# A hybrid decoder layer on one core: projections, pool sums and new tokens laid out anew in the first part

## The chip, the cores and the metric

The kernel runs on one core of a Trainium2 chip. The metric is device time in microseconds, from the start to the end of one execution, lower is better. All data is float32.

## The reference, cut to what matters

One layer for 256 prompt tokens and 8 sample tokens (one new token in each of 8 sequences that have 1024 cached positions):

```python
h = rmsnorm(x, norm_mix)
u, q, k, v, f_logit, g_logit = split(h @ w_in)          # 4 parts of 512 columns, 8 forget columns, 2 x 1024 gates
logf = log_sigmoid(f_logit + b_forget)
pooled[g] = window_sum(u, WINDOWS[g]) / count - u       # windows 2, 4, 8, 16 over time, 128 channels each
pool_out = (pooled @ w_pool) * pool_scale
att = softmax(q k^T / 8 + c_q - c_k, causal) v          # c = cumsum(logf); samples read paged k, v, logf
y = sig(g0) * (pool_out @ w_up_pool) + sig(g1) * (att @ w_up_att)
x = x + y @ w_out
x = x + hier_moe(rmsnorm(x, norm_ffn))                  # 4 groups of 8 experts, top-1 group, top-2 experts
out = rmsnorm(x, norm_final)                            # and new k, v, logf, pool rows
```

The pages of k and v are picked from a cache by a page table: 8 sequences x 8 pages of 128 rows. Each of the 32 experts has three matrices of 2 MB.

## The kernel before, in words

**Storage.** SBUF has a ring of nine slots of 2 MB. In the first part six of them (FRONT) take a stream of 2 MB loads, worked out by a planner: four column blocks of w_in (Q, K, V, U), four gate blocks of w_in, the K and V pages of each sample, w_up_pool, w_up_att and two halves of w_out. Slots 6 to 8 hold activations. SyncE issues weight loads (L485, L489), GpSimd's queue issues the indirect loads of the pages (L562), of the cached forget values (L551), the broadcasts of each sample's query (L574) and most small outputs. Every load waits until the last use of what its slot held.

**Order.** A list PLAN gives one order of steps; each engine runs through it and does its part of each step, in order. Steps: `proj` (L1224 to 1245) multiplies hT (tokens transposed, normalised) with a column block: for each of two blocks of 128 tokens hT is the stationary operand and 512 columns of w_in stream past (L1240); the eight samples are done before with 32 stationary columns in four column groups (L1230), copied by ScalarE and added up by a matmul (L1245). So q, k, v, u come out with tokens on the partitions; `qk` (L1271) transposes q and k back. `forget` (L1250) has 8 stationary columns. `pages` on VectorE sums the cached forget values, `bias` (L1264, L1265, L873) adds the sums over later pages. `keysN` (L879, L883) multiplies two pages of a sample's keys with its query on VectorE and sums over 64 dimensions; four such steps per sample, then L888 to L890. `dmax`, `dshift`, `dsums`, `dpv`, `dsum`, `datt` are the decode softmax of one sample: transpose of the maxima (L1276), shift (L1279, L896), exp (ACT L667), sums (L899), probabilities times V in four column groups (L1286), the new token's V row with 8 contraction rows (L1287), the total (L1290, L901), scaling (L907) and a sum over partitions (L1295). `head` is one prompt head: scores and bias (L1339, L1340), softmax (L923 to L927, ACT L692, L693), transposes of the probabilities of the head before (L1328), `pv` (L1346 to L1348). `pool` makes window sums as matmuls with band matrices (L1306 to L1310) and mixes them (L1314). `gate` (L1320) makes one of 16 tiles of gate logits, `up` and `merge` (L1359) multiply with w_up_pool and w_up_att, `out` (L1368, L1374) with w_out. One turn of the loop over the samples b = 1 to 8 has two gates, one sample's softmax, one head, one `up`.

**After the plan.** `norm` squares x (ACT L618), takes an inverse root in 13 small VectorE operations (L775 to L782), normalises (L786), transposes (L1142, L1145) and multiplies with the router. `route` picks experts; before expert 0 PE also gathers the tokens, and builds tables of slots (L1417, L1422). Then for each expert: gate and up (L1184), turning, down (L1200), combination into PSUM (L1211, L1213). Expert e's loads wait for expert e - 3: w_gate and w_up for its gate and up products (`s_gu`, L452), w_down for its down product (`s_dn`, L454). At the end the rows are squared (ACT L745, L748), a root is taken and two row blocks and the samples are scaled (L1119, L1121) and written (L532, L536).

**Start.** SyncE loads x_sample, small constants (`cea`), x_prompt, then the stream. GpSimd loads the page table in eight small loads that repeat each value on 16 partitions (L547); ScalarE loads the forget weights (L596, 1024 pieces of 32 bytes). x is squared on ScalarE, normalised on VectorE and then transposed on PE.

## Time and profile before

| | us |
|---|---|
| median of 3 runs | 801.41 (799.28 to 801.55) |
| the profiled execution, its own time | 802.27 |
| its span, first to last instruction | 800.5 |
| PE busy | 651.5 (81%) |
| VectorE busy | 250.7 (31%) |
| ScalarE busy | 71.2 (9%) |
| GpSimd busy | 44.6 (6%) |
| moved by DMA | 269.65 MB, mean 337 GB/s |

The times of stages below are offsets from the span's start. A matmul in float32 stands as two records; "x16" are eight matmuls. PEclk is the granted TensorE clock: 1.00 is 2.4 GHz, 0.50 is 1.2 GHz. The span and the execution's own time differ by 1.8 us, which lies around the span.

### The profile page before, as it was taken

To read this page: it belongs to the slowest core of one execution; us is meant where nothing else is said; L and a number is where in the kernel's file an instruction comes from. 1 tells how busy PE (TensorE), PEld (TensorE's weight loads), DVE (VectorE), ACT (ScalarE), POOL (GpSimd) and SP (SyncE) were. 2 spreads that over 40 slices of the span, in tenths; PEclk is the share of its full clock that TensorE was granted. 3 is DMA by queue.
4 is the path that set the end of the run, shared out by engine and by line. 5 is a ranking of instruction groups with operands and counts; after the bars stand their busy time and mean duration, and the time that the engine had idled before them with its cause. 6 is when DMAs were issued, how large, how long until landed. Compare 5 with 4: busy or idle time off the path is not lost.

```text
span 800.5 us, 13635 instructions
## 1 busy us (share of the span) xinstructions
PE 651.5 (81%) x6078; PEld 361.7 (45%) x6078; DVE 250.7 (31%) x634; ACT 71.2 (9%) x182; POOL 44.6 (6%) x55
## 2 busy tenths in 40 slices
PE   1999989999999997899787778677778668778673
PEld 1334476566666635544343344334434334344341
DVE  3104639788782325622111111111111111111103
ACT  2012121111111010100000000000000000000001
POOL 2411111222100000000000000000000000000000
PEclk9999969999999999899988888978978978978887
DMA  5994456978897865099999999999999999999981
GB/s 189 307 388 173 133 225 181 329 266 355 246 369 296 322 251 207 31 366 424 414 424 422 415 423 425 413 423 424 415 421 422 418 421 425 417 418 423 418 362 72
DMA packets 45739, 269.65 MB, mean 337 GB/s; under 512 B 5640, under 2 KB 6456, under 8 KB 35175
## 3 DMA queue, kind: packets, MB, share of 16 engines
q1 hardware_dynamic: 37664, 228.73, 72.0%
q0 software_dynamic: 3968, 37.29, 11.9%
q10 hardware_dynamic: 4047, 2.73, 1.2%
q8 instruction: 50, 0.82, 0.4%
q14 instruction: 10, 0.08, 0.0%
HBM read 266.50 MB, written 2.46 MB: 336 GB/s over the span
## 4 chain that ended last, share of the span: by engine, by line
PE 42%; DMA 36%; SPq 10%; DVE 8%; issue 2%; ACT 1%; DVEq 0%; ACTq 0%
DMA ring<-w_up 34%; PE bank L1184 8%; SPq L452 8%; PE bank L1240 7%; PE bank L1320 4%; PE bank L1374 4%; PE bank L1286 2%; DVE ring L879 2%; PE bank L1359 2%; SPq L516 2%; DVE front L883 1%; DMA x<-x_prompt 1%; PE bank L1230 1%; PE bank L1200 1%; PE bank L1167 1%
## 5 line engine op out<-in xcount | busy, mean ns | idle before, releaser
L1184 PE MATMUL bank<-ring,front 128*32 128x256 f32 x2048 | 168.3, 500 | 100.8 <-DMA ring<-w_up 96.5
L1184 PEld LDWEIGHTS bank<-ring,front 128*32 128x32 f32 x2048 | 91.0, 143 | 170.1 <-issue 147.8
L1065 DVE COPY front<-bank 128x256 f32<-128x256 f32 x32 | 13.6, 424 | 246.4 <-PE bank L1184 246.4
L1320 PE MATMUL bank<-hT,ring 128*128 128x264 f32 x256 | 63.1, 401 | 0.0
L1200 PE MATMUL bank<-ring,front 128*32 128x256 f32 x1024 | 61.1, 379 | 0.7 <-DVE front L1070 0.7
L1240 PE MATMUL bank<-ring,hT 128*128 128x512 f32 x128 | 57.0, 598 | 0.0
L1167 PE MATMUL bank<-front 128*32 128x256 f32 (+1 forms) x768 | 53.0, 390 | 0.8 <-DVE front L981 0.8
L1320 PEld LDWEIGHTS bank<-hT,ring 128*128 128x128 f32 x256 | 48.8, 196 | 9.5 <-issue 1.5
L726 ACT ACTIVATE front<-bank 128x128 f32<-128x128 f32 x32 | 8.9, 278 | 389.3 <-PE bank L1192 389.3
L1200 PEld LDWEIGHTS bank<-ring,front 128*32 128x32 f32 x1024 | 33.2, 110 | 22.7 <-DVE front L1070 0.9
L1075 DVE COPY front<-bank 128x256 f32<-128x256 f32 x32 | 13.6, 425 | 86.5 <-PE bank L1200 86.5
L883 DVE TENSOR_REDUCE front<-ring 128x16 f32<-128x1024 f32 x32 | 39.0, 1220 | 1.1
L879 DVE TENSOR_TENSOR ring<-ring,front 128x1024 f32<-128x1024 f32 x32 | 38.9, 1216 | 0.0
L1240 PEld LDWEIGHTS bank<-ring,hT 128*128 128x128 f32 x128 | 23.7, 190 | 32.7 <-issue 32.7
L1211 PE MATMUL bank<-front 32*128 32x256 f32 x512 | 36.7, 400 | 0.5 <-DVE front L1075 0.5
L1167 PEld LDWEIGHTS bank<-front 128*32 128x32 f32 (+1 forms) x768 | 18.4, 107 | 24.9 <-issue 18.6
L1211 PEld LDWEIGHTS bank<-front 32*128 32x128 f32 x512 | 23.1, 184 | 14.5 <-issue 12.8
L1374 PE MATMUL bank<-ring,hT 128*128 128x512 f32 x64 | 28.3, 597 | 0.0
L1070 DVE TENSOR_TENSOR front<-front,bank 128x128 f32<-128x128 f32 x32 | 9.2, 288 | 46.5 <-ACT front L726 46.5
L1213 PE MATMUL bank<-front 128*32 128x256 f32 x256 | 20.4, 391 | 0.0
L1374 PEld LDWEIGHTS bank<-ring,hT 128*128 128x128 f32 x64 | 11.9, 190 | 16.4 <-issue 16.4
L1286 PE MATMUL bank<-ring,front 128*32 128x512 f32 x128 | 18.4, 701 | 0.0
(262 smaller groups left out, 560.1 us busy)
## 6 DMA issues: line engine op xcount, KB each, us to landing
ring<-w_up SPq DMA_DIRECT2D x31, 2048.0 KB, 30.7
ring<-w_gate SPq DMA_DIRECT2D x31, 2048.0 KB, 34.2
ring<-w_down SPq DMA_DIRECT2D x31, 2048.0 KB, 34.6
ring<-w_in SPq DMA_DIRECT2D x8, 2048.0 KB, 20.6
ring<-w_out SPq DMA_DIRECT2D x2, 2048.0 KB, 10.1
front<-q_scratch POOLq DMA_DIRECT2D x8, 256.0 KB, 6.0
ring<-w_up_pool SPq DMA_DIRECT2D x1, 2048.0 KB, 10.8
ring<-w_up_att SPq DMA_DIRECT2D x1, 2048.0 KB, 15.4
```

The costliest lines, as they stand in the source:

```text
L452: eng.dma_start(slot[q], src.rearrange("e (p k) f -> p (e k f)", p=P)).then_inc(s_slot[q], 16)
L879: v.tensor_tensor(ks, ks, qb[:, a % 2].unsqueeze(1).to_broadcast([P, 2, DC]), ALU.mult).then_inc(s_kprod, 1)
L883: v.tensor_reduce(sc[:, 2 * pair:2 * pair + 2], ks.rearrange("p j (h d) -> p j h d", h=HEADS), AX.X, ALU.add).then_inc(s_kused, 1)
L1167: last = m.matmul(bank[GATHER][CAP * g:CAP * (g + 1), 0:QUART], sel[0:n, i, b], h2[0:n, b, g * QUART:(g + 1) * QUART], start=b == 2, stop= ...
L1184: last = m.matmul(bank[GATEUP][32 * g:32 * g + 32, 0:256], xgT[:, k % 2, k // 2], w[:, k, 256 * (g % 2):256 * (g % 2) + 256], start=k == 0 ...
L1200: last = m.matmul(bank[TDOWN][32 * g:32 * g + 32, 0:256], hE[:, j % 2, j // 2], wd[:, j, 256 * g:256 * g + 256], start=j == 0, stop=j == F ...
L1211: m.matmul(acc[:, g, b], back[rows, i, b * P:(b + 1) * P], ysb[rows, i], start=False, stop=False, skip_group_check=True)
L1213: last = m.matmul(bank[SACC][CAP * g:CAP * (g + 1), 0:QUART], back[:, i, SEQ + CAP * g:SEQ + CAP * (g + 1)], ysb[:, i], start=False, stop= ...
L1240: last = m.matmul(out[:], hT[:, k, b * P:(b + 1) * P], w[:, k], start=k == 0, stop=k == DK - 1)
L1286: m.matmul(out[g:g + 32, :], pex[:, j], pages[:, j], start=j < 4, stop=j >= 4 and j % 4 > 0)
L1320: last = m.matmul(out[:, 0:TOK], w[:, k, cols], hT[:, k, 0:TOK], start=k == 0, stop=k == DK - 1)
L1374: last = m.matmul(out[:], hT[:, k, b * P:(b + 1) * P], w[k // CC][:, k % CC, half * 512:(half + 1) * 512], start=k == 0, stop=k == DK - 1)
```

## The change

- **Projections** use w_in as the stationary operand: for each of four tiles of 128 columns, 8 matmuls stream 264 tokens (prompt and samples together). The result has channels on the partitions. Copies go to qT, kT, uP (also v, for a while) and the samples' part to sT. A new step `nat` brings samples (and K and V of the prompt) into rows again by PE.
- **Start**: x is transposed raw on PE; the root of each row is spread over the partitions by a matmul with a diagonal and multiplied in on VectorE together with norm_mix. The page table comes in one load, spread by a matmul; the forget weights are loaded on SyncE's queue behind K's block. ScalarE's Sqrt starts the root, five VectorE operations finish it. The loads of cached forget values wait for K's block.
- **Forget logits** are made in four column groups and summed by `fsum`.
- **Pool sums** over windows are 16 chained GpSimd operations on uP instead of band matmuls; the copies for the router and three small outputs follow them on GpSimd's queue.
- **Heads** go in pairs (`scores`, `pT`, `pv`), the two of a pair on different row or column groups of PE: scores and softmax of two heads in every odd turn, transposes and `pv` in every even one. ScalarE takes over the copies of `dpv` and `pv`.
- **New tokens** of the samples: products, weights and division for all eight at once (`snew`, `dfin`).
- **Before and after the experts**: the tables of slots come behind expert 0's gate and up products; the samples are combined first; squares are taken by halves while VectorE multiplies with norm_final; ScalarE scales one of two row blocks and issues half of the sample outputs.

The core of the diff:

```diff
-        PLAN = [("proj", C_Q), ("dq", 0), ("dq", 1), ("proj", C_K), ("forget", 0), ("proj", C_V), ("forgetT", 0), ("pages", 0),
-                ("keys0", 0), ("keys1", 0)] + [("qk", i) for i in range(4)] + [
-                ("proj", C_U), ("keys2", 0), ("bias", 0), ("keys3", 0), ("pool", 0), ("dmax", 0)]
-        PLAN += [("pool", g) for g in range(1, CC + 1)]
+        PLAN = [("proj", C_Q), ("nat", C_Q), ("dq", 0), ("dq", 1), ("proj", C_K), ("forget", 0), ("nat", C_K), ("snew", 0), ("fsum", 0), ("keys0", 0),
+                ("proj", C_V), ("forgetT", 0), ("pages", 0), ("nat", C_V), ("keys1", 0), ("keys2", 0), ("bias", 0),
+                ("proj", C_U), ("keys3", 0), ("nat", C_U), ("pool", 0), ("dmax", 0)]
         for b in range(1, NS + 1):
-            now = b < NS
-            PLAN += [("hnorm", b - 2)] * (b > 1) + [("dq", b + 1)] * (b + 1 < NS) + [("keys0", b)] * now
-            PLAN += [("gate", 2 * b - 2), ("dshift", b - 1)] + [("keys1", b)] * now + [("dsums", b - 1), ("head", b - 1), ("dpv", b - 1)]
-            PLAN += [("keys2", b)] * now + [("dsum", b - 1), ("gate", 2 * b - 1)] + [("keys3", b)] * now
-            PLAN += [("datt", b - 1)] + [("up", b - 1), ("dmax", b)] * now + [("pv", b - 2)] * (b > 1)
-        PLAN += [("hnorm", HEADS - 1), ("head", HEADS), ("up", DK - 1), ("pv", HEADS - 1)]
+            now, c = b < NS, (b - 1) // 2
+            PLAN += [("dq", b + 1)] * (b + 1 < NS) + [("keys0", b)] * now
+            PLAN += [("gate", 2 * b - 2), ("dshift", b - 1)] + [("keys1", b)] * now + [("dsums", b - 1)]
+            PLAN += [("scores", c)] * (b % 2) + [("pT", c)] * (1 - b % 2) + [("dpv", b - 1)]
+            PLAN += [("keys2", b)] * now + [("hnorm", c)] * (b % 2) + [("gate", 2 * b - 1)] + [("keys3", b)] * now
+            PLAN += [("datt", b - 1)] + [("pv", c)] * (1 - b % 2)
+            PLAN += [("mix", g) for g in range(CC)] * (b == 1) + [("up", b - 1)] + [("dmax", b)] * now
+        PLAN += [("dfin", 0)]
         PLAN += [("merge", n) for n in range(DK)] + [("out", 0), ("norm", 0), ("route", 0)]
...
                     sp.dma_start(dst.rearrange("p (k n) -> p k n", k=DK),
                                  w_in[:, first:first + DC].rearrange("(p k) n -> p k n", p=P)).then_inc(done, 16)
+                    if item == ("w", C_K):
+                        sp.wait_ge(s_pad, 4)
+                        sp.dma_start(wf[:, :, 0:HEADS], w_in[:, W_FORGET:W_FORGET + HEADS].rearrange("(p k) n -> p k n", p=P)).then_inc(in_wf, 16)
                 else:
...
+                ins = g.memset(tile[:, :, 0:PAD], 0.0)
+            ins.then_inc(s_zero, 1)
             pool.wait_ge(s_ridx, 1)
+            pool.wait_ge(s_slot[where["w", C_K]], 16)
...
+                elif step == "pool":
+                    pool.wait_ge(*count_taken("proj", C_U, CC - 1))
+                    pool.wait_ge(in_pool, 16 * 4)
+                    now = slice(PAD, PAD + SEQ)
+                    link(g.tensor_tensor(winA[:, :, now], uP[:, :, now], uP[:, :, PAD - 1:PAD - 1 + SEQ], ALU.add))
+                    link(g.tensor_tensor(winB[:, :, now], winA[:, 1:, now], winA[:, 1:, PAD - 2:PAD - 2 + SEQ], ALU.add))
+                    link(g.tensor_tensor(winA[:, 2:, now], winB[:, 1:, now], winB[:, 1:, PAD - 4:PAD - 4 + SEQ], ALU.add))
+                    link(g.tensor_tensor(winB[:, 2, now], winA[:, 3, now], winA[:, 3, PAD - 8:PAD - 8 + SEQ], ALU.add))
+                    for n in range(CC):
+                        win = (winA[:, 0], winB[:, 0], winA[:, 2], winB[:, 2])[n]
+                        link(g.tensor_tensor(win[:, PAD:PAD + PLEN], win[:, PAD:PAD + PLEN], C["fix"][:, n, 0:PLEN], ALU.mult))
+                        link(g.tensor_scalar(win[:, now], win[:, now], 1.0 / WINDOWS[n], None, ALU.mult))
+                        g.tensor_tensor(pooledT[:, n, 0:SEQ], win[:, now], uP[:, n, now], ALU.subtract).then_inc(s_pooled, 1)
+                    pool.wait_ge(*count_taken("last"))
+                    g.dma_start(t["new_pool_prompt"][0, 0], unew[0:PLEN]).then_inc(out_tok, 16)
+                    pool.wait_ge(*count_taken("natS", C_U))
+                    g.dma_start(t["new_pool_sample"][0, :, PLEN - 1, :], samp[96:96 + NS]).then_inc(out_pool, 16)
+                    g.dma_start(t["new_pool_sample"][0, :, 0:PLEN - 1, :], t["state_pool"][0, :, 1:PLEN, :]).then_inc(out_pool, 16)
+                    pool.wait_ge(in_route, 16 * 5)
...
         @block.scalar
...
+            act.wait_ge(s_pad, 2)
+            s.activation(warm, eps, ACT.Sqrt)
+            for b, n in ((0, P), (2, NS)):
                 act.wait_ge(*((in_xs, 16) if b == 2 else (in_xp, 16)))
                 mean_square(b, n, sqout)
+            act.wait_ge(s_sqd, 1)
+            square_root(slice(0, 3), 2)
             act.dma_start(cla[:], t["c_late"]).then_inc(in_cl, 16)
-            act.dma_start(nffn[:], t["norm_ffn"][0].rearrange("(p k) -> p k", p=P)).then_inc(in_route, 16)
-            act.dma_start(wre[:], t["w_router_expert"][0].rearrange("g (p k) e -> p g (k e)", p=P)).then_inc(in_route, 16)
...
+                elif step == "dpv":
+                    src = full("dpv", a)
+                    if a:
+                        act.wait_ge(*count_full("datt", a - 1))
+                    s.copy(mk, src[:]).then_inc(taken[PART], 1)
...
         @block.vector
...
+            def roots(blocks, squares, count):
+
+                a, r, t2 = rowsq[:, blocks], root[:, blocks], rowt[:, blocks]
+                dve.wait_ge(s_sq, squares)
+                dve.wait_ge(s_rt, count)
+                link(v.tensor_scalar(a, a, EPS, -0.5, ALU.add, ALU.mult))
+                link(v.reciprocal(r, r))
+                link(v.tensor_tensor(t2, r, r, ALU.mult))
+                link(v.tensor_tensor(t2, t2, a, ALU.mult))
+                return v.scalar_tensor_tensor(r, t2, 1.5, r, ALU.add, ALU.mult)
...
+            for k in range(DK):
+                dve.wait_ge(s_xT, 1 + k // 2)
+                src = bank[XBANK[k // 2]][:, (k % 2) * SEQ:(k % 2 + 1) * SEQ]
+                v.scalar_tensor_tensor(hT[:, k, 0:SEQ], src, nmix[:, k:k + 1], rootB[:, 0:SEQ], ALU.mult, ALU.mult).then_inc(s_hT, 1)
...
                         v.tensor_copy(attT[:, :, SEQ + a], full("datt", a)[:, 0:CC]).then_inc(taken[CHAIN], 1)
+                    elif step == "dfin":
...
+                        dve.wait_ge(*count_taken("datt", NS - 1))
+                        for f in range(2):
+                            r = slice(HD * f, HD * f + HD)
...
+                            if a:
+                                dve.wait_ge(*count_full("pT", a - 1, f))
+                            else:
+                                dve.wait_ge(*count_full("forgetT"))
...
+            for half in (1, 0):
+                if half == 0:
+                    dve.wait_ge(s_sq, 8)
+                qs = slice(2 * half, 2 * half + 2)
+                v.tensor_tensor(ysq[:, qs], acc[:, qs], nfq[:, qs].unsqueeze(2).to_broadcast([P, 2, PB, QUART]), ALU.mult).then_inc(s_prod, 1)
...
         @block.tensor
...
-
-                    out = free("part", a)
-                    if a == C_Q:
-                        pe.wait_ge(*count_taken("hT", 0, 0))
+                    for n in range(CC):
+                        out = free("proj", a, n)
+                        for k in range(DK):
+                            if a == C_Q and n == 0:
+                                pe.wait_ge(s_hT, max(k, 1) + 2)
+                            last = m.matmul(out[:, 0:TOK], w[:, k, n * P:(n + 1) * P], hT[:, k, 0:TOK], start=k == 0, stop=k == DK - 1)
...
+                    for n in range(CC):
+                        last = m.matmul(out[g:g + NS, n * P:(n + 1) * P], sT[:, a, n], ident, start=True, stop=True)
...
+                        last = m.matmul(out[g:g + 32, 0:TOK], wf[:, k], hT[:, k, 0:TOK], start=k < 4, stop=k >= 4)
...
-                    m.matmul(out[0:32, :], pex[0:NS, PAGES], samp[0:NS, C_V], start=False, stop=True).then_inc(filled[PART], 1)
-                    out = free("den", a)
-                    pe.wait_ge(s_psm, a + 1)
-                    m.matmul(out[:, 0:1], psm, ones[:, 0:1], start=True, stop=True).then_inc(filled[CHAIN], 1)
...
+                    for b, cols in ((0, slice(0, P)), (1, slice(P, 3 * P))):
+                        n = (b + 1) * P
+                        for f in range(2):
+                            r = slice(HD * f, HD * f + HD)
+                            m.matmul(outs[f][:, cols], qT[r, a, b * P:(b + 1) * P], kT[r, a, 0:n], start=True, stop=False)
...
+                else:
+                    list_slots()
+                    pe.wait_ge(*count_taken("tables"))
                 turn_hidden(e)
```

## Rows read from the trace of the kernel before

**Rows 1.** The page: the DMA traffic in GB/s in 40 slices.
```profile
GB/s 189 307 388 173 133 225 181 329 266 355 246 369 296 322 251 207 31 366 424 414 424 422 415 423 425 413 423 424 415 421 422 418 421 425 417 418 423 418 362 72
```
**Rows 2.** Windows: length, busy PE, PEld, DVE, ACT, POOL, clock, DMA share, GB/s.
```profile
255.00:341.15 86.15, 75.68 (x428) 45.18 (x428) 35.78 (x116) 7.18 (x13) 0.00 (x0) 0.96 0.54 209
341.15:778.77 437.62, 337.16 (x4534) 176.71 (x4535) 64.92 (x218) 20.15 (x62) 0.00 (x0) 0.86 1.01 417
```
**Rows 3.** Timeline around expert 0: start, length, engine, line.
```profile
332.98 3.67 PE L1422 MATMUL bank<-part,hT 128*32 128x64 f32 x48
...
337.42 3.66 PE L1184 MATMUL bank<-ring,front 128*32 128x256 f32 x64 [0.78 <-DVE hT L1041]
...
341.15 0.33 SPq L452 DMA_DIRECT2D ring<-w_gate  x1
```
**Rows 4.** Chain of waits at the start: start, length, what.
```profile
1.59 9.82 DMA x<-x_prompt
...
26.76 6.87 PE bank L1240 x16
```
**Rows 5.** SyncE's first load of w_in, issued at 2.05 us.
```profile
DMA to landing us min/median/max: 20.1/20.1/20.1
```
**Rows 6.** Windows at the start (columns as in rows 2).
```profile
6.00:8.00 2.00, 0.00 (x0) 0.00 (x0) 0.00 (x0) 0.00 (x0) 0.24 (x1) 1.00 0.82 312
8.00:10.00 2.00, 0.00 (x0) 0.00 (x0) 0.00 (x0) 0.00 (x0) 0.00 (x0) 1.00 0.23 71
```
**Rows 7.** Timeline: the `merge` step, 32 matmuls of 264 columns.
```profile
259.24 14.48 PE L1359 MATMUL bank<-ring 128*128 128x264 f32 x64 [0.61 <-DVE ring L930]
```
**Rows 8.** The same view: transposes of `qk`, samples' part of a projection.
```profile
41.58 1.92 PE L1230 MATMUL bank<-ring,hT 128*32 128x512 f32 x16
...
79.34 1.09 PE L1271 MATMUL bank<-cea,ring 128*128 128x128 f32 x8
```
**Rows 9.** One line's instructions: a GpSimd copy of 256 elements (ns min/median/max).
```profile
L554 POOL COPY wr<-wre x1: 413/413/413, 39.1 to 39.1; 128x256 f32<-128x256 f32 x1
```
**Rows 10.** Windows: `pool` steps, first turn, fifth turn (columns as in rows 2).
```profile
100.00:113.00 13.00, 10.66 (x47) 9.72 (x47) 5.89 (x10) 2.67 (x7) 3.71 (x5) 0.65 0.78 309
...
113.40:131.50 18.10, 17.88 (x80) 12.04 (x80) 10.89 (x19) 3.79 (x9) 2.38 (x2) 0.88 0.25 87
...
185.40:202.80 17.40, 17.17 (x90) 11.53 (x89) 14.96 (x27) 2.46 (x8) 2.79 (x3) 1.00 0.93 376
```
**Rows 11.** Timeline: a wait of PE at 101 to 103 us; the fifth turn.
```profile
103.33 0.27 PE L1276 MATMUL bank<-cea,front 128*8 128x128 f32 x1 [2.34 <-DVE front L890]
...
185.35 3.83 PE L1320 MATMUL bank<-hT,ring 128*128 128x264 f32 x16
...
187.69 1.22 DVE L883 TENSOR_REDUCE front<-ring 128x16 f32<-128x1024 f32 x1
...
191.35 0.69 PE L1340 MATMUL bank<-front,cea 8*128 8x256 f32 x2
...
193.83 1.04 PE L1287 MATMUL bank<-front 8*32 8x512 f32 x2
...
197.69 0.74 DVE L907 SCALAR_TENSOR_TENSOR front<-bank,stat,cla 128x512 f32<-128x512 f32 x1
```
**Rows 12.** The load of gate block 1, issued at 130.50 us.
```profile
DMA to landing us min/median/max: 15.7/15.7/15.7
```
**Rows 13.** Timeline: the root of the second block of rows.
```profile
311.03 0.14 DVE L775 TENSOR_SCALAR rowsq<-rowsq 128x1 f32<-128x1 f32 x1
...
313.52 1.31 DVE L786 TENSOR_SCALAR front<-x,root 128x1024 f32<-128x1024 f32 x1
```
**Rows 14.** Timeline: the end.
```profile
787.67 0.38 ACT L745 ACTIVATE front<-bank 128x256 f32<-128x256 f32 x1 [4.64 <-PE bank L1213]
...
794.03 2.48 DVE L1119 SCALAR_TENSOR_TENSOR x<-bank,root,x 128x1024 f32<-128x1024 f32 x2
...
796.93 1.70 SPq L536 DMA_DIRECT2D y_sample<-front  x4
```

790 lines of the change are left out of this document (431 added, 359 removed).

## The prediction

> **What bounds the kernel now.** I read the page first, then windows of its two halves, then the chain of waits and timelines. From 341 us on the DMA engines are full: 437.6 us at 417 GB/s with a share of 1.01, while PE has 337 us of work [rows 2]. This stretch is the 29 experts from 3 to 31, 15.1 us each. It begins when expert 0's gate and up products end, at 341.15, because SyncE then issues expert 3's loads [rows 3]. Before that the traffic is far lower, and nothing at all is moved just ahead of 341 (31 GB/s in the slice 320 to 340, [rows 1]). So the kernel is: a first part bound by its compute chain, then a fixed stretch of DMA, then a tail. What the first part loses in time the end gains in full, as long as its 85 MB (the first 17 slices of [rows 1] times 20 us) still fit: at 417 GB/s they need 205 us, and I forecast a restart near 301.
>
> Sum against the profiled execution's 802.27 us (span 800.5, 1.8 around it); the median of the runs shown is 801.41, 0.86 lower.
>
> **1. Start, -11.3 us.** Prompt products begin at 26.76 [rows 4]. x lands at 11.41 [rows 4], w_in's first block at 2.05 + 20.1 = 22.15 [rows 5], although the engines move 312 GB/s at 6 to 8 us and only 71 at 8 to 10 [rows 6], in the time in which the small pieces of the page table and the forget weights are under way. The change takes those out of the way. I take x's landing at 8.0. Then: two squares on ScalarE 2.5, square root 0.3, five VectorE operations 1.0, diagonals 0.8, spreading matmul 0.6, copy 0.4, three products 1.1, sum 6.7: 14.7. The weight block, 2.1 MB at 390 GB/s (about what flowed at 16 to 24) behind x, lands near 13.5. With handovers 15.5. Bounds: 12.5 (x at 6.5) and 22.2 (block as late as now).
>
> **2. Projections and what lies to gate 0, -14.1 us.** Now from 26.76 to gate 0 at 113.4 [rows 4, 10]: 86.7 us, PE busy nearly throughout. After, per projection 32 matmuls of 264 columns; `merge` has exactly that, 14.5 us [rows 7]; four make 58.0. (Now 7.1 + 7.1 + 1.9 + 1.0 = 17.1 each.) Added PE work: four `nat` of the samples, 1.6 each with the wait for ScalarE's copies, 6.4; two times eight transposes at 1.1 [rows 8], 2.2; the forget logits in four column groups, half of the 1.9 that the samples' 512 columns take [rows 8], 1.0; `fsum`, `snew`, `forgetT`, `bias` with two waits of 0.7, 3.3; the last rows of u and the four state matmuls 1.4; `dmax` 0.3. Sum 72.6. The band matmuls go (pool stage: 13 us at a clock of 0.65, [rows 10]). Gate 0 then starts at 15.5 + 72.6 = 88.1. Added waits: `forget` on SyncE's forget weights, 1024 small pieces behind K's block, needed at 45 us; the cached forget values behind K's block, eight issues from about 20 us on, done by 31, earlier than the key pages go out now. Both are covered by K's projection; uncovered they cost what they are late.
>
> **3. Pool sums on GpSimd, 0.** The trace shows no arithmetic on GpSimd but a copy of 256 elements in 0.413 us, 1.6 ns each [rows 9]. The sums are some 4,670 elements per partition: 7.5 us by that rate. Lower end 5.6 (VectorE's 1.22 us per 1024, [rows 11]), upper end 15 (two inputs, twice the copy's rate). They start at 84 us and PE wants them for `mix` near 102: the first turn covers all of it. Their queue matters more: three small outputs, the router copies and then the broadcast of query 2 stand behind them. Issued near 98, landing 6 to 11 us later, it is wanted at 106: 0 to 3 us late, I take 0.
>
> **4. The loop, -8.8 us.** Now a full turn is 17.4 us at full clock with PE busy 17.2 [rows 10]; from gate 0 to `merge` 113.4 to 259.24 is 145.8 [rows 7, 10]. PE per turn after: gone are the new token's V row 1.0 [rows 11] and the total 0.24. The score matmuls (a head's four take 2.07; the last is 0.69, [rows 11]) stand for two heads side by side: bounds 2.1 (fully parallel) and 4.1 per pair; I take 2.1, since expert products on four row groups lie close to parallel in this trace. `pv` 1.1 per pair for 1.6; `datt` in 64-column tiles 1.6 for 0.8 (bounds 0.8 to 2.2). An even turn is then 15.5 us of PE. An odd turn has only 14.5 of PE, but VectorE now has both heads in it: from one `dmax` to the next `dmax` 0.5, keys 4 x 2.45 (two operations of 1.22, [rows 11]) = 9.8, wait for gate and shift 1.2, shift 0.14, sums 0.3, two heads 2.8, `hnorm` 1.2, closing 0.8, `datt` and `up` 0.6: 17.4. The scaling of 0.74 [rows 11] and the `pv` copy of 0.42 have gone to ScalarE, which is idle most of the turn. So pairs alternate: odd turns stay as they are with VectorE as bound, even ones fall to 15.5. Four odd 69.6, three even 46.5, the last turn 12.7, then `pv`, `up`, the total and a wait for `dfin`'s eight operations 5.2: 134.0; plus 3.0 for stretches at the lower clock as today. The pages: gate block 1 needs 15.7 us to land [rows 12] and would have one even turn, 15.5 plus 0.7; just enough. `merge` starts at 225.1, 34.1 earlier.
>
> **5. To the restart, -6.0 us.** The second row block's root takes 311.03 to 313.52 [rows 13]; with ScalarE's root and five operations 1.0 instead of 2.5: -1.5. The first root is hidden by `out`. Moving the slot tables behind expert 0's products: they took 332.98 to 337.42 [rows 3], -4.5. Their 4.5 us then lie between expert 0's products and its down products, so w_down of expert 3 is issued 9 us after the restart instead of 4; w_gate and w_up fill those 9 to 10 us. Cover gone, up to 4 us come back.
>
> **6. Tail, -3.8 us.** From 787.67 [rows 14]: root two thirds shorter, squares beginning earlier, -1.7; the two multiplications of 2.48 together [rows 14] become one of 1.2 beside ScalarE's, -1.2; half of the four issues of 1.70 [rows 14] go to ScalarE, -0.9.
>
> Sum: 11.3 + 14.1 + 8.8 + 6.0 + 3.8 = 44.0. 802.27 - 44.0 = 758.3; against the median 757.4. **Forecast 757.5**, own range 750 to 765.
>
> **The rivals.**
> *The start does not move forward.* w_in's first block stays the last to land: 6.7 us come back, 764. For it: 2 MB behind x in a queue that was slow for 8 us. Against: [rows 6] tie the slowness to the small pieces. Chance 0.13.
>
> *GpSimd in VectorE's way.* The loss would be in the first turn: if each of VectorE's operations waits for a GpSimd sum or the other way round, the 7.5 us of sums (15 at most) are laid end to end with VectorE's keys, and query 2 comes 3 to 5 us late; VectorE sets odd turns. About +9: 766. The trace has no overlap of GpSimd arithmetic with VectorE, so it speaks neither way. Chance 0.12. The Trainium skill has this rule (SBUF — State Buffer, Who interferes with whom): a VectorE instruction with two SBUF inputs and a GpSimd instruction that reads SBUF block each other through a shared read port. By that rule this rival holds at least in part; no row here can show it. The same skill (GPSIMD Engine Reference, Elementwise) gives 4497 ns for an addition of 2048 float32, 2.2 ns an element; as an estimate by that page the sums take 10 us.
>
> *The loop packs better.* `datt` at 0.8, VectorE's waits hidden, later landings no matter, restart undisturbed: 8 us less, 749. Chance 0.17.
>
> *The clock drops in odd turns.* PE waits about 2.5 us in one piece for VectorE before `dmax`. The one such wait now is 2.34 us and ends at 103.33 [rows 11]; around and behind it the clock is 0.65 and then 0.88 for a turn [rows 10], that is 13 us at 1.2 GHz. If every odd turn brings 7 such microseconds: 4 x 3.5 = +14, 771. Chance 0.11.
>
> *Slower.* The same wait, but the clock stays at 1.2 GHz through the loop: PE's 15 us per turn become 30, eight turns 240 instead of 137, +103: 861. It decides from 44 us of doubled PE work on, three turns. For it: one wait of this kind cost 13 us of clock, almost a turn. Against: among the experts PE waits each time for DMA and the mean clock is still 0.86 [rows 2]. Chance 0.04.
>
> *Nothing gained*, because earlier loads only meet a full DMA sooner: needs 205 us of traffic to bind before 301; 0.01.
>
> The forecast itself has 0.42. Own bounds of the sum (start -3.0/+6.7, loop -6/+8, `forget` waits +3) with the rivals of both sides give **744 to 776**, leaving out the slow end, the case of nothing gained and a little at each end. A measurement of this kernel can tell about 0.3% (2.4 us) from no change. Faster 0.95, within it 0.01, slower 0.04.
>
> **What would show it.** In the changed profile: first product near 15.5; gate 0 near 88; loop turns alternating 17.4 and 15.5 with a wait of PE for VectorE only in odd ones; `merge` near 225; expert 3's loads issued near 301; then 437.6 us as now; tail of 18 us instead of 21.7. Wrong if the stretch after the restart is longer (then DMA was not the fixed part), if PE waits for ScalarE's copies in `nat` by more than 0.7 each, if K or V pages land late in even turns, or if GpSimd's sums take over 18 us, for then `mix` stands in PE's way.

## The result, and the profile after

The kernel after takes **774.37 us** (median of 4 runs, 771.85 to 779.07); the kernel before took 801.48 beside it (4 runs, 799.28 to 805.49). The ratio is 0.9654, with a 95% interval of 0.9614 to 0.9694. Forecast were 757.5 and a range of 744 to 776: the sign and the range held, and the point was 17 us too low. The profiled execution took 774.42 us, its span is 772.5, 28.0 less than before.

The page, the traffic in 40 slices, answers to [rows 1], and the share of GpSimd is new to it:

```profile
POOL 0503381121000000000000000000000000000000
GB/s 217 284 382 262 151 171 294 373 353 310 377 348 293 338 108 139 241 415 425 420 415 424 422 418 420 424 420 419 421 421 419 421 423 418 422 420 419 421 376 94
```

The hole of 31 GB/s ahead of the expert stream has become three thinner slices (108, 139, 241). Windows, columns as in [rows 2]: from `merge` to the restart of the weight loads, from there to the last weights' product, and the first, second and fourth turn of the loop:

```profile
232.12:312.38 80.26, 72.44 (x359) 40.02 (x359) 29.39 (x87) 10.04 (x18) 0.00 (x0) 0.91 0.53 210
312.38:753.28 440.90, 335.96 (x4588) 184.23 (x4589) 67.68 (x227) 20.15 (x62) 0.00 (x0) 0.86 1.00 414
...
92.11:114.30 22.19, 18.77 (x100) 12.43 (x100) 17.11 (x35) 6.37 (x17) 20.11 (x25) 0.89 0.62 213
114.30:136.03 21.73, 17.43 (x91) 11.44 (x91) 11.56 (x18) 2.75 (x7) 3.19 (x4) 0.80 0.85 291
...
152.50:166.20 13.70, 13.70 (x91) 9.79 (x91) 11.29 (x18) 2.82 (x7) 3.56 (x4) 1.00 0.88 306
```

The stretch that I called fixed is 440.90 us against 437.62 [rows 2]. The first two turns take 22 us each, forecast at 17.4 and 15.5, while an undisturbed even turn is better than forecast (13.7 for 15.5).

The start, TensorE's timeline and windows (answering to [rows 4, 6]). TensorE waits 6.51 us for the query columns of w_in, which land 16.5 us after their issue at 2.10; [rows 5] had 20.1:

```profile
18.70 17.18 PE L1377 MATMUL bank<-hT,ring 128*128 128x264 f32 x64 [6.51 <-DMA ring<-w_in]
...
109.02 0.76 PE L1463 MATMUL bank<-front,ring 128*128 128x264 f32 x2 [2.31 <-issue]
...
124.45 3.64 PE L1446 MATMUL bank<-ring,front 128*32 128x512 f32 x16 [4.30 <-issue]
...
232.12 16.17 PE L1515 MATMUL bank<-ring 128*128 128x264 f32 x64 [2.75 <-DVE ring L1017]
...
306.52 5.79 PE L1301 MATMUL bank<-ring,front 128*32 128x256 f32 x64 [0.58 <-DVE front L1097]
...
319.02 0.66 PE L1309 MATMUL bank<-cea,front 128*128 128x128 f32 x2 [3.71 <-DVE front L1172]
```

```profile
8.00:10.00 2.00, 2.00 (x11) 1.81 (x9) 0.50 (x3) 1.20 (x3) 0.00 (x0) 1.00 1.00 152
...
14.00:16.00 2.00, 0.00 (x0) 0.00 (x0) 2.00 (x6) 0.00 (x0) 0.00 (x0) 0.50 0.99 146
...
18.00:20.00 2.00, 1.30 (x3) 1.13 (x4) 0.00 (x0) 0.00 (x0) 0.00 (x0) 0.50 1.04 406
```

The DMA engines are fully busy from 8 to 16 us, but move only 146 to 189 GB/s in each stretch of 2 us; at 18 us they move 406 with the same share. The other lines of the first fence are the waits in the first two turns (L1463 is `mix`, L1446 the page products of `dpv`), `merge` at 16.17 us for 14.48 [rows 7], gate_up(0) at 5.79 us for 3.66 [rows 3], and the wait behind the tables.

GpSimd's timeline in the first turn. [rows 9] was all that the trace before had of its arithmetic:

```profile
92.28 1.91 POOL L613 TENSOR_TENSOR ring<-ring 128x1024 f32<-128x1024 f32 x1
94.28 2.41 POOL L614 TENSOR_TENSOR ring<-ring 128x768 f32<-128x768 f32 x1
96.76 2.02 POOL L615 TENSOR_TENSOR ring<-ring 128x512 f32<-128x512 f32 x1
...
104.27 0.85 POOL L620 TENSOR_SCALAR ring<-ring 128x256 f32<-128x256 f32 x1
...
106.19 1.92 POOL L620 TENSOR_SCALAR ring<-ring 128x256 f32<-128x256 f32 x1
108.19 0.72 POOL L621 TENSOR_TENSOR front<-ring 128x256 f32<-128x256 f32 x1
...
111.04 0.60 POOL L597 DMA_DIRECT2D front<-q_scratch  x1
```

VectorE's timeline in the same stretch:

```profile
92.78 1.45 DVE L998 TENSOR_SCALAR front<-cea,stat 8x8 f32<-8x8 f32 x1
94.15 1.21 DVE L984 TENSOR_TENSOR ring<-ring,front 128x1024 f32<-128x1024 f32 x1
...
96.66 1.22 DVE L984 TENSOR_TENSOR ring<-ring,front 128x1024 f32<-128x1024 f32 x1
...
106.19 1.21 DVE L984 TENSOR_TENSOR ring<-ring,front 128x1024 f32<-128x1024 f32 x1
...
121.43 1.23 DVE L984 TENSOR_TENSOR ring<-ring,front 128x1024 f32<-128x1024 f32 x1 [6.15 <-DMA front<-q_scratch]
```

The sums take 92.28 to 108.91, 16.6 us. Behind them stand three outputs and two router copies, and only at 111.04 the broadcast of query 2, for which VectorE waits 6.15 us. SyncE's timeline at the restart (answering to [rows 3]) has w_down of expert 3 issued 13.0 us behind w_gate; in the kernel before it was 4.3 behind (345.42 for 341.15). First the kernel after, then the kernel before:

```profile
312.38 0.33 SPq L466 DMA_DIRECT2D ring<-w_gate  x1
...
325.39 0.38 SPq L468 DMA_DIRECT2D ring<-w_down  x1
```
```profile
345.42 0.38 SPq L454 DMA_DIRECT2D ring<-w_down  x1
```

### The profile page after: what moved, and what is told of

Its sections match the earlier page's. It is cut to its first block, busy times and chain, and to the rows that moved or that the text cites. A ratio compares the mean times of both kernels' runs of the same rounds, so it can differ in the third digit from the quotient of the medians.

```text
span 772.5 us, 13852 instructions
## 1 busy us (share of the span) xinstructions
PE 614.4 (80%) x6169; PEld 375.2 (49%) x6169; DVE 233.0 (30%) x603; ACT 85.8 (11%) x231; POOL 52.7 (7%) x66
## 4 chain that ended last, share of the span: by engine, by line
DMA 40%; PE 39%; SPq 9%; DVE 7%; issue 3%; ACT 1%; DVEq 0%; ACTq 0%
DMA ring<-w_up 36%; PE bank L1301 9%; PE bank L1377 8%; SPq L466 8%; PE bank L1469 5%; DMA ring<-w_in 4%; PE bank L1530 4%; PE bank L1515 3%; DVE ring L984 1%; PE bank L1284 1%; PE bank L1317 1%; SPq L532 1%; PE bank L1446 1%; DVE front L988 1%; PE bank L1332 1%
## 5 line engine op out<-in xcount | busy, mean ns | idle before, releaser
L1377 PE MATMUL bank<-hT,ring 128*128 128x264 f32 x256 | 60.6, 400 | 6.5 <-DMA ring<-w_in 6.5
L1469 PE MATMUL bank<-hT,ring 128*128 128x264 f32 x256 | 62.7, 399 | 2.3 <-DMA ring<-w_in 2.3
L1377 PEld LDWEIGHTS bank<-hT,ring 128*128 128x128 f32 x256 | 50.3, 197 | 16.0 <-issue 6.9
L1469 PEld LDWEIGHTS bank<-hT,ring 128*128 128x128 f32 x256 | 48.8, 196 | 18.7 <-issue 7.8
L1284 PE MATMUL bank<-front 128*32 128x256 f32 (+1 forms) x768 | 54.9, 401 | 0.8 <-DVE front L1088 0.8
L984 DVE TENSOR_TENSOR ring<-ring,front 128x1024 f32<-128x1024 f32 x32 | 38.9, 1217 | 6.2 <-DMA front<-q_scratch 6.2
L1284 PEld LDWEIGHTS bank<-front 128*32 128x32 f32 (+1 forms) x768 | 18.7, 109 | 26.3 <-issue 20.3
L1332 PEld LDWEIGHTS bank<-front 32*128 32x128 f32 x512 | 23.1, 184 | 13.9 <-issue 13.2
L1530 PE MATMUL bank<-ring,hT 128*128 128x512 f32 x64 | 28.3, 597 | 0.0
L1446 PE MATMUL bank<-ring,front 128*32 128x512 f32 x128 | 17.1, 656 | 4.7 <-issue 4.3
L1326 PE MATMUL bank<-front 128*32 128x256 f32 x256 | 20.1, 379 | 0.5 <-DVE front L1182 0.5
L1530 PEld LDWEIGHTS bank<-ring,hT 128*128 128x128 f32 x64 | 11.9, 190 | 16.4 <-issue 16.4
```

Of the source, the lines that this page charges most:

```text
L984: v.tensor_tensor(ks, ks, qb[:, a % 2].unsqueeze(1).to_broadcast([P, 2, DC]), ALU.mult).then_inc(s_kprod, 1)
L1284: last = m.matmul(bank[GATHER][CAP * g:CAP * (g + 1), 0:QUART], sel[0:n, i, b], h2[0:n, b, g * QUART:(g + 1) * QUART], start=b == 2, stop= ...
L1332: last = m.matmul(acc[:, g, b], back[rows, i, b * P:(b + 1) * P], ysb[rows, i], start=False, stop=False, skip_group_check=True)
L1377: last = m.matmul(out[:, 0:TOK], w[:, k, n * P:(n + 1) * P], hT[:, k, 0:TOK], start=k == 0, stop=k == DK - 1)
L1446: last = m.matmul(out[g:g + 32, :], pex[:, j], pages[:, j], start=j < 4, stop=j >= 4)
L1469: last = m.matmul(out[:, 0:TOK], w[:, k, cols], hT[:, k, 0:TOK], start=k == 0, stop=k == DK - 1)
```

## The experiments

Each starts from the kernel after. Where a run is set against "after", that is 774.37 us, and "gate 0" is the start of the first gate step, "the restart" the issue of expert 3's w_gate, "the stream" the time from there to the last weights' product. Executions of one kernel scatter by some us, and the intervals of runs 1 to 3 and 5 to 8 overlap with that of after (0.9614 to 0.9694), run 5's just so; what a single edit gives is therefore read from its trace, and the median stands beside it. Medians of the kernel before beside the runs were 800.53 to 802.22.

**1. Tables back ahead of the experts.**
```
+            list_slots()
+            pe.wait_ge(*count_taken("tables"))
             for e in range(EXPERTS):
...
-                else:
-                    list_slots()
-                    pe.wait_ge(*count_taken("tables"))
```


> One part undone: the tables' products and the wait for their copy stand ahead of the expert loop again, the rest stays as in the kernel after. My theory (the restart comes earlier but w_down(3) then waits longer, and the gap is a bubble of the weights' stream): first w_gate of expert 3 issued 3.5 to 4.5 us later after the routing (313.5 to 317), w_down(3) then 4 to 5 us behind it instead of 13.0, last weights' product 437 to 438 us behind the restart instead of 440.9; net 0 to +1.5 us on 774. Rival (the prediction's own term, the restart is worth what it is moved by): +4 to +4.5 us. Second rival (moving the tables behind expert 0 costs more than it gives): -1 us or less.

Measured: 776.95 us (ratio to before 0.9671, 0.9602 to 0.9739). From `out`'s end to the restart 3.1 us longer, and w_down(3) 4.3 us behind it. SyncE and the last weights' product:
```profile
316.52 0.33 SPq L466 DMA_DIRECT2D ring<-w_gate  x1
...
320.80 0.38 SPq L468 DMA_DIRECT2D ring<-w_down  x1
```
```profile
754.23 1.93 PE L1301 MATMUL bank<-ring,front 128*32 128x256 f32 x32 [1.63 <-DMA ring<-w_up]
```
754.23 - 316.52 = 437.7, again the 437.6 of before. The move gave 3.1 us at the restart and the stream paid 3.2 for it: net nothing. The spans differ by 1.0, which is the start of this execution (first product 19.7 for 18.7). The median is 2.6 over after, above the expected 0 to 1.5.

**2. Broadcast of query 2 ahead of the sums.**
```
-                ("proj", C_U), ("keys3", 0), ("nat", C_U), ("pool", 0), ("dmax", 0)]
+                ("proj", C_U), ("keys3", 0), ("nat", C_U), ("dq", 2), ("pool", 0), ("dmax", 0)]
...
-            PLAN += [("dq", b + 1)] * (b + 1 < NS) + [("keys0", b)] * now
+            PLAN += [("dq", b + 1)] * (2 < b + 1 < NS) + [("keys0", b)] * now
```


> One entry of the order of work is moved: the broadcast of query 2 stands ahead of the pool sums in GpSimd's queue instead of behind them. Theory (the broadcast was late because it stood behind the sums, the outputs and the router copies): it lands before 100 us, VectorE's wait of 6.15 us ahead of the first key products of query 2 and TensorE's gap of 4.27 us at 120 us vanish, merge begins 4 to 6 us earlier (226 to 228 instead of 232.1), the whole 768 to 771. Rival (the turn is bound elsewhere, by VectorE's chain or by gate block 1, and the gap only moves): merge less than 2 us earlier, the whole within 2 us of 774.

Measured: 770.17 us (0.9592, 0.9511 to 0.9672). The wait of 6.15 us is gone, VectorE's first key product of query 2 starts at 115.98 instead of 121.43:
```profile
115.98 1.20 DVE L984 TENSOR_TENSOR ring<-ring,front 128x1024 f32<-128x1024 f32 x1
```
The second turn fell from 21.7 to 15.6 us, the first rose by 1.1; `merge` starts at 226.85, 5.3 earlier. The queue behind the sums cost 5 us; the first turn, with the sums still at 16.6 us, stays long.

**3. Products in the wait of the start.**
```
             last.then_inc(s_rB, 1)
+            for _ in range(12):
+                m.matmul(bank[PART], ident, x[:, 0:PB, 0:QUART], start=True, stop=True)
```


> Added: 12 products of 128x512 into an unused bank between the products that spread the roots and the first projection, where TensorE waits 6.5 us for the first weights. Theory (the wait is what lets the granted clock fall at 13.9, and the Q projection pays 2.7 us for it): the clock stays up, the Q projection takes 14.5 us instead of 17.2, first product at 18.6 to 19.0, the whole 2 to 3 us shorter. Rival (the clock falls for what came before, or for the power of the start, whatever TensorE does in the wait): Q projection 17 us, the whole unchanged or up to 0.5 longer.

Measured: 778.62 us (0.9685, 0.9613 to 0.9757), 4.3 over after where 2 to 3 less were expected: the fill was too long (10.46 us into a wait of 6.5), so the first projection starts at 22.44. But it runs at full clock:
```profile
12.14 10.46 PE L1368 MATMUL bank<-x,cea 128*128 128x512 f32 x24
22.44 14.40 PE L1379 MATMUL bank<-hT,ring 128*128 128x264 f32 x64
```
14.40 us for 17.18: the granted clock of 14 to 16 us is 1.00 where it was 0.50. What the low clock behind the wait costs is shown (2.8 us). The first product came 3.7 us later, so this edit made the start 1.0 us longer; `merge` starts 3.6 us later. The other 2.6 came in the loop: in this execution two gate steps, behind waits of 2.06 and 1.94 us, ran at the low clock, see below.

**4. Another column block first.**
```
-                    first = a * DC if kind == "w" else W_GATE + a * DC
+                    first = (1, 0, 2, 3)[a] * DC if kind == "w" else W_GATE + a * DC
```


> Only the source addresses of the first two loads of w_in are exchanged, so that the key columns go where the query columns went and the reverse; queries and keys are therefore exchanged in what is computed, and only the first 40 us are read. Theory A (the first load is slow because it is the first, beside the other loads of the start): first load lands at 18 to 19 us, the second 6 us later, as now. Theory B (the slow rate belongs to the column block, as the even blocks at 6 to 16 and at 26 to 34 us ran at half the rate of the odd ones): first load lands at 12 to 14 us, the second takes 10 to 12 us and lands at 23 to 25; the first product at 15 to 16 as forecast.

The text above names the wrong block: w_in's columns stand in the order u, q, k, v, so what the edit exchanged is the query columns with the pool input's columns (loaded last), and the key columns stayed second. So queries and pool inputs are exchanged in what is computed. One execution was measured (772.12 us): the first load lands at 14.8 instead of 18.6, the second (the keys) at 20.9. From 6 to 12 us the engines move 350 to 358 GB/s, in the time in which they moved 152 to 233, although the small pieces of the forget weights are issued at the same place (3.50 us).
```profile
14.94 17.19 PE L1377 MATMUL bank<-hT,ring 128*128 128x264 f32 x64 [1.95 <-DVE hT L913]
```
TensorE now waits for hT alone. The slowness goes with the columns, not with the place in the queue and not with the small pieces. That 17.19 is still the low clock (0.50 from 14 to 20 us), although the wait was only 1.95 us.

**5. Pool sums on VectorE.** The block of sums is moved word for word from GpSimd's `pool` step to VectorE's:
```
-                    link(g.tensor_tensor(winA[:, :, now], uP[:, :, now], uP[:, :, PAD - 1:PAD - 1 + SEQ], ALU.add))
+                        link(v.tensor_tensor(winA[:, :, now], uP[:, :, now], uP[:, :, PAD - 1:PAD - 1 + SEQ], ALU.add))
...
```


> The pool sums alone go from GpSimd to VectorE, same operations and same operands, at the same place in the order of work. Theory (on GpSimd they took 16.6 us and held up the mix products and, behind them in its queue, the broadcast of query 2): on VectorE they take 7 to 8 us, mix's wait of 2.3 us at 106.7 and the wait of 6.15 us for the broadcast vanish; the first turn's VectorE work starts 6 to 8 us later, but the first turn ends 2 to 5 us earlier; merge at 227 to 230 instead of 232.1, the whole 769 to 772. Rival (VectorE is the bound of the first turn, so what GpSimd spends beside it is cheaper than 7.5 us on VectorE): merge at 233 to 238, the whole 775 to 780.

Measured: **766.52 us** (0.9571, 0.9509 to 0.9634), 7.9 under after. VectorE's timeline:
```profile
89.70 1.23 DVE L966 TENSOR_TENSOR ring<-ring 128x1024 f32<-128x1024 f32 x1 [7.33 <-ACT front L691]
...
96.47 0.43 DVE L974 TENSOR_TENSOR front<-ring 128x256 f32<-128x256 f32 x1
...
97.47 0.22 DVE L999 TENSOR_SCALAR front<-cea,stat 8x8 f32<-8x8 f32 x1
```
The same sums take 7.2 us, 2.7 of them in a wait that VectorE had anyway. `merge` starts at 224.3, 7.8 earlier than in the kernel after: a larger gain than the expected 227 to 230 (and 769 to 772 for the whole). Nor does it lie where I expected it:
```profile
92.37:114.60 22.23, 19.80 (x100) 12.22 (x100) 19.10 (x49) 6.34 (x17) 5.89 (x9) 0.85 0.86 329
114.60:128.30 13.70, 13.70 (x92) 9.80 (x91) 11.54 (x18) 2.82 (x7) 3.58 (x4) 1.00 1.03 232
```
The first turn is as long as in after (22.2), since VectorE now does the sums ahead of its own part. The second falls from 21.7 to 13.7, 2 us more than in run 2, as it runs at full clock. The same operation of 8 elements that took 1.45 us beside GpSimd's takes 0.22 here.

**6. Tables behind expert 0.**
```
                 if e < LAST:
                     turn_tokens(e + 1)
+                if e == 0:
+                    pe.wait_ge(s_ysb, 1)
+                    list_slots()
```
and on VectorE the tables' copy and `return_map(0)` behind `rows(0)` and `turned(1)`.

> The tables' products stand behind the down product of expert 0 and the turning of its successor's tokens, instead of between gate_up(0) and down(0), and VectorE takes the tables after those; same work. Theory (w_down(3) was issued 13.0 us behind the restart because the tables stood in its way, and the hole in the weights' stream is carried to the end): w_down(3) 4 to 6 us behind the restart, w_gate(4) 10 to 14 behind it, the last weights' product 437 to 438.5 us behind the restart instead of 440.9, the whole 771 to 772. Rival (the hole is hidden, the 440.9 has another cause): restart to last product unchanged, the whole 774.

Measured: 772.65 us (0.9643, 0.9582 to 0.9705). SyncE and the last weights' product:
```profile
310.72 0.33 SPq L466 DMA_DIRECT2D ring<-w_gate  x1
...
315.00 0.38 SPq L468 DMA_DIRECT2D ring<-w_down  x1
322.04 0.33 SPq L466 DMA_DIRECT2D ring<-w_gate  x1
```
```profile
748.73 1.93 PE L1307 MATMUL bank<-ring,front 128*32 128x256 f32 x32 [0.47 <-DMA ring<-w_up]
```
748.73 - 310.72 = 438.0. The restart keeps its earlier place and the stream gets its 437.6 back, although the next w_gate still comes 11.3 us behind (8.9 before): it is w_down's delay that made the hole. The median gained 1.7 us (772.65, just outside the expected 771 to 772), less than the 2.9 of the stream and within the scatter of the two.

**7. Fillers in the routing.**
```
+                    hold(2)
                     out = free("ranks")
...
+                    hold(1)
                     pe.wait_ge(*count_taken("ranks"))
...
                     gather(0)
+                    hold(1)
                     turn_tokens(0)
+                    hold(1)
```
where `hold(n)` is n products of `x` with the unit matrix into the bank of gate_up.

> Added: five products of 128x512 into the unused bank of gate_up in the gaps of the routing (two ahead of the ranks, one behind them, one ahead of and one behind the turning of expert 0's tokens). Theory (small products and gaps of 1 us in the routing let the granted clock fall at 300.6, and gate_up(0) pays 2.1 us for it): clock up through gate_up(0), which takes 3.7 us instead of 5.8, restart 1 to 2 us earlier, less up to 1 us by which the fillers delay the chain. Rival (the clock falls anyway): gate_up(0) at 5.8 and the restart 0.3 to 1.5 us later.

Measured: 773.32 us (0.9636, 0.9577 to 0.9695). The clock stayed up and gate_up(0) took 3.66 us; from `out`'s end to the restart 27.0 us instead of 29.2. The median shows 1.0 of it, because this execution's loop was 3 us longer than that of after:
```profile
151.62 0.27 PE L1436 MATMUL bank<-cea,front 128*8 128x128 f32 x1 [2.07 <-DVE ring L1007]
151.75 5.49 PE L1469 MATMUL bank<-hT,ring 128*128 128x264 f32 x16
...
310.20 3.66 PE L1301 MATMUL bank<-ring,front 128*32 128x256 f32 x64 [0.59 <-DVE front L1097]
```
The gate step behind the 2.07 us wait takes 5.49 us here; in the kernel after, behind the same wait, 3.80. And with the clock up through gate_up(0), w_down(3) is still issued 13.0 us behind the restart (326.88 for 313.92).

**8. Heads of a pair in turn.** The loops over f (head) and b (rows) of the score products are exchanged:
```
-                    for b, cols in ((0, slice(0, P)), (1, slice(P, 3 * P))):
...
-                        for f in range(2):
+                    for f in range(2):
+                        for b, cols in ((0, slice(0, P)), (1, slice(P, 3 * P))):
```


> The four score steps issue the same 8 products head by head instead of alternating between the two row halves of the array. Theory (products of 64 rows in different halves run beside each other only when they stand next to each other): a score pair takes 3.2 to 4 us instead of 2.1, TensorE's busy time is 4 to 8 us higher in the loop, and since the odd turns wait for VectorE the whole is 0 to 4 us longer. Rival (the pair's price is by bytes or columns, whatever the order): 2.1 us, nothing changes.

Measured: 779.03 us (0.971, 0.9648 to 0.9772), 4.7 over after, where 0 to 4 were expected, with a pair of 3.2 to 4 us; both are a little over. The first score step, of the kernel after and then of this one:
```profile
96.08 0.49 PE L1480 MATMUL bank<-ring 64*128 64x128 f32 x4
...
98.18 1.92 PE L1446 MATMUL bank<-ring,front 128*32 128x512 f32 x16
```
```profile
95.15 0.49 PE L1480 MATMUL bank<-ring 64*128 64x128 f32 x2
...
99.31 1.92 PE L1446 MATMUL bank<-ring,front 128*32 128x512 f32 x16
```
From the start of the pair to the page products behind it 2.10 us against 4.16: two products (four records) in the 0.49 us of one when the halves of the array alternate, and no overlap when they don't.

**9. Four edits together**, 5, 6, 7 and 3 with 7 products in place of 12.

> Four edits together, all tried alone before: pool sums on VectorE, tables behind expert 0, five products in the gaps of the routing, and products in the wait ahead of the first projection, 7 instead of the 12 that overran it. If the parts add (each sits in a stage of its own): merge at 222 to 225, gate_up(0) at 3.7 us, w_down(3) 4 to 6 us behind the restart, 774.4 - 7.9 (sums) - 2.3 (tables) - 2.2 (routing) - 2.5 (start) = 759.5, range 757 to 763. Rival (they share one gain, as the low clock that each of them avoids comes back elsewhere): 764 to 768.

Measured: **759.91 us** (0.948, 0.9439 to 0.9522); forecast 759.5. Q projection 14.48 us, `merge` at 222.2, w_down(3) 4.3 us behind the restart, gate_up(0) 3.66 us, 437.5 us of stream. By stages the parts add. The medians of the single runs would not have said so (7.9, 1.7 and 1.0 us gained, and 4.3 lost by the fill of 12): the forecast took the sizes of the last three from their traces.

**10. The same, keys first.** `("proj", C_K)` stands ahead of `("proj", C_Q)` in the order, with the two waits that depend on it, and 2 fill products.

> As the run before, but the key columns of w_in are loaded and projected first and the query columns second, and the wait has 2 fill products instead of 7. Theory (it is the query columns' load that is slow, wherever it stands, and behind the key projection of 14.5 us it is hidden): first load lands at 14 to 16, first product at 15 to 16, no gap between the first two projections; if the clock stays up 3 to 4 us shorter than the run before, 755 to 758; if it falls, 757 to 760. Rival (what is first is slow): first load at 18 to 19, no gain.

Measured: 758.56 us (0.9461, 0.9418 to 0.9504). The clock stayed up and the first product is at 16.05, but the expected 755 to 758 were missed: TensorE waits 3.12 us at 49.4 for the forget bias, gate 0 is at 91.3, and the time can't be told from run 9's.

**11. Keys first alone.**

> The kernel after with the order of the first two blocks alone exchanged, keys first, and nothing added. Theory: first load lands at 14 to 16 instead of 18.6, first product 3 to 4 us earlier than 18.7, gate 0 at 87 to 90 instead of 92.1; the first projection at the lower clock. Rival (what is first is slow): first load at 18 to 19, gate 0 at 92.

One execution was measured: 778.04 us. In runs 10 and 11 the first load landed at 13.5 and 14.0 and the query columns were hidden behind the keys' projection, and in both the gain went at once. TensorE in run 11:
```profile
14.71 31.09 PE L1377 MATMUL bank<-hT,ring 128*128 128x264 f32 x128 [1.68 <-DVE hT L913]
...
50.53 1.99 PE L1412 MATMUL bank<-hT,wf 128*32 128x264 f32 x16 [3.16 <-DMA bf<-b_forget]
```
A first product 4.0 us earlier, and a wait of 3.16 us for the forget bias, which ScalarE issues behind the query projection, now the second. Gate 0 at 92.3, as in after. Expected were 87 to 90: missed, for a load that I had not followed.

**12. The same with that load early.**
```
-                    if a == C_Q:
+                    if a == C_K:
                         late_loads()
```
on top of run 10.

> As the run of the four edits with the keys first, but ScalarE issues the forget bias and the pool's constants behind the first projection, as the kernel after does, and not behind the second. Theory (in that run TensorE's 3.12 us at 49.4 for the bias took back what the earlier start gave): no wait for the bias, gate 0 at 86.5 to 88 instead of 91.3, the whole 754 to 757 instead of 758.6. Rival (the gain is taken back by another late load, or by the page loads that these now stand beside): gate 0 at 89 to 91, the whole 757 to 760.

Measured: **756.45 us** (0.9412, 0.9363 to 0.9461), the best version: 5.9% under before, 2.3% under after. TensorE, then a window of the weight stream:
```profile
14.33 28.72 PE L1386 MATMUL bank<-hT,ring 128*128 128x264 f32 x128 [0.31 <-DMA ring<-w_in]
```
```profile
297.72:735.23 437.51, 331.58 (x4588) 181.68 (x4589) 67.51 (x226) 20.16 (x62) 0.00 (x0) 0.86 1.01 417
```
The first two projections together take 28.7 us at full clock; gate 0 is at 86.8 (86.5 to 88 expected; the prediction had 88.1), the restart at 297.7 (301).

## Why the forecast was right, and where it was 17 us short

The range held, with 1.6 us to spare, and in part by luck: in the loop a miss of 11 us met a gain of 8 that I had not forecast (points 3 and 4); without that gain the time would have lain above 776. By its own terms, profiled execution against profiled execution (spans 800.5 and 772.5, so 28.0 gained for 44.0 forecast):

| term | forecast | measured | how |
|---|---|---|---|
| 1 start | -11.3 | -8.1 | 26.76 to 18.70 |
| 2 projections | -14.1 | -13.2 | 86.6 to 73.4 |
| 3, 4 sums and loop | -8.8 | -5.8 | 145.8 to 140.0 |
| 5 to the restart | -6.0 | -1.6 | 81.9 to 80.3 |
| 5 stream, "up to 4 come back" | 0 | +3.3 | 437.6 to 440.9 |
| 6 tail | -3.8 | -2.5 | 21.7 to 19.2 |

**1. Start, mis-sized by 3.2.** x came early (6.5 for 8.0) and hT was ready near 16. The step that failed is "2.1 MB at 390 GB/s": I blamed [rows 6]'s low traffic on small pieces. Runs 4 and 11 show that it is the query columns themselves: moved to another place, they are slow there, and another block lands at 14.0 to 14.8. This is the rival "the start does not move forward", to half its price.

**2. Projections, right but for the clock.** 73.4 us for 72.6 (the 86.7 of the sum is 86.64, so the term was -14.0). The query projection alone lost 2.7 to the low clock; so the rest was 1.9 under its sum. Run 3 shows that the clock follows the wait: filling it brings 14.40.

**3. Pool sums, "7.5 us, upper end 15, cost 0": this failed most, and the first two turns were 4.8 and 6.2 us over the forecast's.** They took 16.6 us, above my upper end. By rows there are two parts. GpSimd alone needs 1.87 ns an element at 1024 elements, and 0.73 to 0.85 us for 256, twice the copy that I had scaled from. And where its operation stood beside a two-input operation of VectorE, one waited for the other: L620 takes 1.92 us beside L984 at 106.19 and 0.85 else, L998 1.45 for 0.22. All four lengthened sums (L614, L615, one of L621, one of L620) overlap with an L984 (at 94.15, 96.66, 102.14 and 106.19), and L984 itself kept its 1.21 to 1.27. By the Trainium skill (SBUF — State Buffer, Who interferes with whom) such pairs block each other through a shared port; the trace agrees, with these numbers. From the rows L614, L615, L620 and L621 I put this contention at about 3.5 us of the 16.6, an estimate; no run took it away alone, and what it cost the first turn is not shown, for in run 5, where GpSimd has no sums at all, that turn is as long (22.2). The dearer thing was the queue: "0 to 3 us late, I take 0" was 6.15. Run 2 gives 5.3 us back at `merge` by the queue alone, run 5 gives 7.8 by taking the sums off GpSimd. The rival "GpSimd in VectorE's way" (766, chance 0.12) had both parts, engines that wait for each other and a late query 2; its 9 us stand against 11.0, and of these the 6.2 of the second turn are the late query and the low clock behind TensorE's wait for it (21.7 us, 15.6 in run 2, 13.7 in run 5). Of the first turn's 4.8, 2.3 are `mix`'s wait, which ends behind the last sum (109.02 behind 108.91), and 1.8 the low clock behind it (`up` takes 3.86 us at 110.44, 2.05 at 134.00). Without the 3.5 us of contention the sums would have been done before that wait, but no run shows it.

**4. The other six turns were better than forecast**, by 8 us, and that hid most of the 11. The score pair is 2.10 us as taken, because the halves alternate (run 8). `datt` takes 0.63 (1.6 forecast, under my lower bound of 0.8), `pv` 0.85 (1.1). An even turn is 13.7 us (15.5), an odd one 16.5 (17.4). "Just enough" for gate block 1 was so; block 2 came late by 2.28 us at the end of the sixth turn.

**The clock in odd turns.** TensorE waits 2.06 us ahead of `dmax`, as said. In after the clock stayed at 1.00 behind it at 152 and 182; in runs 3, 4, 6, 7, 11 and 12, behind the same 2.06 us, the gate step of the fourth turn took 5.49 us for 3.80 and the turn 15.4 to 15.5 us for 13.7. The wait for gate block 2 did the same in runs 3, 7 and 9 (5.51). So the rival "the clock drops in odd turns" was too dear with 3.5 us per turn: it is 1.7, in one or two turns of a run. That this makes up a good part of the scatter of the times is not shown, since one execution of each kernel was traced.

**5. Restart.** The root gave its 1.5 (285.59 to 286.55 for [rows 13]'s 2.49). The tables gave 4.4 of the place, but gate_up(0) cost 2.1 more and `merge` 1.7 more, both at the low clock; with 0.4 that I did not follow, -1.6 was left. Then the cover: I wrote that w_down of expert 3 would be issued 9 us after the restart and that w_gate and w_up fill 9 to 10. It was 13.0: the tables' products took 3.1 us, VectorE's table operations stood ahead of `hidden` (3.7 us of wait for 0.55), and behind this wait the turning and the down product ran at the low clock (2.94 and 3.00 us for 1.64 and 1.91 in run 1). The hole of 3.3 us is carried to the end; runs 1, 6, 9, 10 and 12 all have 437.5 to 438.0 where w_down comes 4.3 us behind, and the seven others, where it comes 12.1 to 13.3 us behind, have 439.9 to 441.7. Not its own term but its order was wrong: the tables belonged behind `down`, not behind `gate_up`.

**6. Tail, 1.3 short.** ScalarE squares four blocks one behind the other (762.08 to 764.98), its multiplication takes 1.15 us where VectorE's takes 0.75, and SyncE's last two issues 1.76 us where I took half of 1.70.

## What to carry to other kernels

Work that is moved to an idle engine also moves into its queue: follow what stands behind it there, and who waits for that, before it is costed at nothing. Once a stretch is bound by DMA, what counts is when each load of the ring is issued, not only the first; move small work behind the product that frees the next buffer. And a wait of TensorE of some us can cost twice, itself and the clock behind it; a few idle products kept the clock up in two places here, in the wait of the start and in the routing.

## What the runs showed of the hardware that I had not expected

Loads of w_in of the same form (2 MB in 2,048-byte pieces, rows 16,416 bytes apart) ran at two rates by their columns. In stretches of 2 us in which mostly one block was under way, blocks 0 and 2 (u, k) moved at 300 to 410 GB/s, blocks 1 and 3 (q, v) at 145 to 210, with the DMA share near 1.0 in both. The rate went with the columns when the order was changed (runs 4, 11). Why was not tried.

The low clock behind a wait was no fixed price. Behind waits of 6.5 to 6.75 us (after, runs 1 and 5) the first projection took 17.1 to 17.5 us, behind 5.6 to 6.05 (runs 2, 6, 7 and 8) 16.05 to 16.6, against 14.4 when the wait was filled; but run 4 paid 17.19 behind 1.95. And behind the same 2.06 us ahead of `dmax` the gate step took 3.80 us at some turns and 5.49 at others, so that executions of the same code differ by some us without any difference in what they wait for.

And the granted clock of the profile does not always tell it. A stretch of run 6 and one of run 3:
```profile
20.00:22.00 2.00, 2.00 (x6) 1.54 (x5) 0.00 (x0) 0.00 (x0) 0.00 (x0) 1.00 1.06 401
```
```profile
24.00:26.00 2.00, 2.00 (x10) 1.71 (x9) 0.00 (x0) 0.00 (x0) 0.04 (x1) 1.00 1.07 275
```
Both stand at 1.00, yet run 6 has 6 records of the same product in 2 us, as many as after has at 0.50 in its stretch from 20 to 22, and run 3 has 10. So the pace of like products has to be read beside the clock.
